# Column-tiled square sums with tokens on partitions, quartered input and transposed output in a two-layer streaming encoder

## What is computed

```python
def rmsnorm(x, g):
    y = x * lax.rsqrt(jnp.mean(x * x, axis=-1, keepdims=True) + EPS)
    return y * g

def ffn_half(x, g, wg, wu, wd):
    h = rmsnorm(x, g)
    return x + 0.5 * ((jax.nn.silu(h @ wg) * (h @ wu)) @ wd)

def layer(h, ...):
    h = ffn_half(h, n1, w1g, w1u, w1d)
    z = rmsnorm(h, nm) @ w_in
    m, st = token_mix(z, ...)      # chunk MLP, window attention, latent attention
    h = h + m @ w_out
    return ffn_half(h, n2, w2g, w2u, w2d), st
# two layers, then y = rmsnorm(h, norm_final)
```

## Time and profile before

| | |
|---|---|
| runs | 2149.73, 2156.65, 2157.35 us; median 2156.65 |
| the profiled execution's own time | 2156.49 us |
| its span, first to last instruction | 2154.7 us |
| mean granted TensorE clock | 0.992 of full |
| busy: PE, DVE, ScalarE, POOL | 97%, 65%, 43%, 26% |

### The profile page before, as it was taken

How to read it: one execution, slowest core, us unless ns; L and a number is a source line. 1 busy time by engine, 2 the same in 40 slices (tenths; PEclk the granted TensorE clock), 3 DMA queues, 4 the chain that set the end, 5 groups by cost and what they waited for, 6 DMA issues and landing times.

```text
span 2154.7 us, 40797 instructions
## 1 busy us (share of the span) xinstructions
PE 2094.6 (97%) x15625; PEld 2021.1 (94%) x15625; DVE 1410.2 (65%) x2115; ACT 917.7 (43%) x1654; POOL 562.7 (26%) x308
## 2 busy tenths in 40 slices
PE   8999999999998999999989999999999899999999
PEld 7999999998777999999989999999987799999998
DVE  7899961145646899972289999312465479999511
ACT  6444442224535544453255555322244364444411
POOL 2222223341112222223322221333312022222231
PEclk9999999999998999999999999999999999999999
DMA  4323323431112232322223332224222023332322
GB/s 127 98 79 96 95 74 85 110 90 44 42 42 79 68 92 94 97 81 81 75 79 98 97 97 76 81 84 115 69 56 52 30 61 96 97 97 76 91 83 70
DMA packets 250467, 175.37 MB, mean 81 GB/s; under 512 B 35408, under 2 KB 245552, under 8 KB 250352
## 3 DMA queue, kind: packets, MB, share of 16 engines
q1 hardware_dynamic: 248272, 170.09, 26.9%
q10 hardware_dynamic: 2080, 3.67, 0.5%
HBM read 170.12 MB, written 3.62 MB: 81 GB/s over the span
## 4 chain that ended last, share of the span: by engine, by line
PE 88%; DVE 6%; ACT 4%; issue 2%; DMA 0%; ACTq 0%; DVEq 0%
PE pair L1228 42%; PE pair L1179 36%; PE pair L1259 3%; PE pair L1434 1%; PE pair L1269 1%; ACT probs L1089 1%; ACT hidden_high L883 1%; DVE top L2013 1%; PE pair L1425 1%; PE pair L1420 1%; PE pair L1413 1%; PE pair L1376 1%; ACT square L762 1%; DVE t_parts L1870 0%; PE pair L1516 0%
## 5 line engine op out<-in xcount | busy, mean ns | idle before, releaser
L1228 PE MATMUL pair<-t_parts,chunk_high 128*128 128x288 f32 x4592 | 918.0, 296 | 8.7 <-DVE outputs L1680 5.6
L1228 PEld LDWEIGHTS pair<-t_parts,chunk_high 128*128 128x128 f32 x4592 | 738.9, 189 | 9.9 <-issue 7.0
L1228 PE MATMUL pair<-t_parts,chunk_low 128*128 128x288 f32 x2296 | 678.5, 296 | 0.0
L712 POOL TENSOR_TENSOR w_low<-raw,w_high 128x1024 fp32r<-128x1024 f32 (+1 forms) x128 | 294.2, 2308 | 772.6 <-ACT w_high L755 641.4
L1228 PEld LDWEIGHTS pair<-t_parts,chunk_low 128*128 128x128 f32 x2296 | 432.6, 188 | 0.0
L718 POOL TENSOR_TENSOR chunk_low<-set_raw,chunk_high 128x512 fp32r<-128x512 f32 x164 | 237.6, 1459 | 701.7 <-ACT chunk_high L807 701.7
L807 ACT ACTIVATE chunk_high<-chunk_sum 128x512 fp32r<-128x512 f32 x328 | 204.3, 631 | 388.3 <-DVE chunk_sum L1599 188.5
L1179 PE MATMUL pair<-hidden_high,w_high 128*128 128x288 f32 x1408 | 303.1, 297 | 6.6 <-DVE hidden_low L1805 6.2
L1179 PE MATMUL pair<-hidden_low,w_high 128*128 128x288 f32 x1408 | 301.4, 296 | 0.0
L1179 PE MATMUL pair<-hidden_high,w_low 128*128 128x288 f32 x1408 | 301.3, 296 | 0.0
L1565 DVE SCALAR_TENSOR_TENSOR outputs<-pair,rms 128x576 f32<-128x576 f32 x32 | 24.2, 758 | 371.2 <-PE pair L1179 371.2
(11 more groups left out here) (252 smaller groups left out, 2793.6 us busy)
## 6 DMA issues: line engine op xcount, KB each, us to landing
set_raw<-in_w_up_dram SPq DMA_DIRECT2D x44, 1024.0 KB, 5.3
set_raw<-in_w_gate_dram SPq DMA_DIRECT2D x44, 1024.0 KB, 5.3
raw<-in_w_down_dram SPq DMA_DIRECT2D x64, 512.0 KB, 3.8
raw<-in_w_down_dram SPq DMA_DIRECT2D x32, 384.0 KB, 3.5
raw<-in_w_in_dram SPq DMA_DIRECT2D x20, 512.0 KB, 3.9
raw<-in_w_in_dram SPq DMA_DIRECT2D x16, 256.0 KB, 3.8
raw<-in_w_out_dram SPq DMA_DIRECT2D x8, 512.0 KB, 3.5
raw<-in_w_out_dram SPq DMA_DIRECT2D x16, 256.0 KB, 4.1
```

The costliest lines, as they stand in the source:

```text
L712: nc.gpsimd.tensor_tensor(**low_of(s, slot_size(s))).then_inc(low_ready, 1)
L1228: mm = nc.tensor.matmul(out, c[:, j, p, :], tr[p // 2][:, p % 2, x, t, :], start=p == 0 and n == 0, stop=p == KP - 1 and n == 2)
```

## The change

- The mean square of a plain opening is made with 32 weight columns in each product. Square m goes to rows 32 (m mod 3) to 32 (m mod 3) + 31 of pair 3, so three partial sums lie in 96 rows. It now comes after tile (0,1). ScalarE copies the 96 rows to `rms`, and after tile (1,0) PE sums them with tokens on the partitions (5 products with one moving column into pair 0).
- Root and reciprocal are taken on `root_tok` [128, 5]. ScalarE's `spread` scales the identity by each token's value into `sq_tmp`, PE multiplies by `mean_d` (`FIRST` pair, or ALONE in layer 1's first phase), and `keep_scale` copies the result to `rms`, times 1024.
- `make_rms` becomes `make_scale` and moves in DVE's order. DVE waits for `rms_spread` before its first use of `rms`. In the normal opening `mean_square` is one step, `spread_scale` follows S4 and A22 of set (0,1), and set (1,0) waits for `rms_spread` at A11; `after_plain` now holds for plain phases only.
- The low parts of weight tiles (0,0), (1,0), (1,1) move from POOL to DVE (`plain_chunk_low`); POOL only passes the counts on. Tile (0,0) takes its records pair by pair.
- x comes in four quarters, the sample rows in one transfer on SP's queue; ScalarE copies h's even tiles whole, DVE the odd ones; w_up's load waits for the third quarter, w_gate's for the fourth. Three fp32 products of `sq_sum` (zeros) run on PE ahead of the transposes.
- DVE multiplies the last h by the gain into `y_in`, and `y_chunk` is a plain transpose; `diag` goes.

```diff
+            sp.dma_start(x_tok[0:DEC, 4, :], a["x_sample"][0]).then_inc(x_sample_in, 16)
...
-                    sp.wait_ge(x_in[0], 32)
+                    sp.wait_ge(x_in[2], 16)
...
-                        sp.wait_ge(xT_done, KD)
+                        sp.wait_ge(x_in[3], 16)
...
                 for n in range(2):
+                    if b == 0 and n == 0:
+                        pool.wait_ge(plain_low, 3 * plain_before(layer, w) + 1)
+                        pool.sem_inc(low_by_pool, 1)
+                        continue
+                    if b == 1:
+                        pool.wait_ge(plain_low, 3 * plain_before(layer, w) + n + 2)
+                        pool.wait_ge(low_by_pool, 2 * q + n)
+                        pool.sem_inc(low_by_pool, 1)
+                        continue
                     pool.wait_ge(chunk_high, 7 * q + (3, 7)[n])
...
-                    nc.scalar.activation(rms[:, half * HALF:(half + 1) * HALF], ps[ALONE][:, 1, 0:HALF], ACT.Sqrt,
-                                         bias=eps[:, 0:1]).then_inc(root_done, 1)
+            def root(count, sums, parts):
+                act.wait_ge(sum_done, 2 * count + 2)
+                nc.scalar.activation(root_tok[:, 0:4], sums[:, 0:4], ACT.Sqrt, bias=eps[:, 0:1], scale=float(parts)).then_inc(root_done, 1)
+                nc.scalar.activation(root_tok[0:DEC, 4:5], sums[0:DEC, 4:5], ACT.Sqrt, bias=eps[0:DEC, 0:1], scale=float(parts)).then_inc(root_done, 1)
+            def spread(count):
+                act.wait_ge(rms_ready, count + 1)
+                for t, (t0, n) in enumerate(TILES):
+                    ins = nc.scalar.activation(sq_tmp[0:n, t0:t0 + n], ident[0:n, 0:n], ACT.Copy, scale=root_tok[0:n, t:t + 1])
+                ins.then_inc(spread_made, 1)
+            def keep_scale(ph, part, pair, half):
+                act.wait_ge(scale_made, 2 * ph + part + 1)
+                dst, src = (rms[:, 0:SEQ], ps[pair][:, 0, :]) if part == 0 else (rms[:, SEQ:NT], ps[pair][:, half, 0:DEC])
+                nc.scalar.activation(dst, src, ACT.Copy, scale=float(D_MODEL)).then_inc(rms_spread, 1)
             def gate_up(layer, w, base_slot):
                 ph = 2 * layer + w
...
                     for j in (S1, S2, S3, S4):
                         chunk(q + 1, 1 - b, j)
+                        if opens and b == 1 and j == S1:
+                            spread(3 * layer + 2 * w)
+                        if opens and b == 1 and j == S4:
+                            keep_scale(ph, 0, ALONE, 0)
                     done(A22)
                     chunk(q + 1, 1 - b, A22)
+                    if opens and b == 1:
+                        keep_scale(ph, 1, ALONE, 0)
                 if is_plain(layer, w):
...
+                keep_up(0)
                 combined_of(0)
+                act.wait_ge(sum_done, 2 * ph + 1)
+                nc.scalar.activation(two(rms[0:96, :]), halves(3)[0:96], ACT.Copy).then_inc(parts_kept, 1)
...
-                keep_up(0)
+                keep_up(1)
                 combined_of(2)
+                root(ph, ps[ALONE][:, 0, 0:5], D_MODEL // 32)
                 combined_of(3)
-                act.wait_ge(sum_done, 2 * ph + 2)
-                nc.scalar.activation(two(rms[:, :]), halves(3), ACT.Sqrt, bias=eps[:, 0:1]).then_inc(root_done, 2)
+                spread(3 * layer + 2 * w)
                 chunk(q + 2, 0, A11)
                 chunk(q + 2, 0, A12)
-                keep_up(1)
-                for j in (S1, S2, S3, S4):
+                for j in (S1, S2):
+                    chunk(q + 2, 0, j)
+                keep_scale(ph, 0, FIRST, 0)
+                keep_scale(ph, 1, FIRST, 1)
+                for j in (S3, S4):
                     chunk(q + 2, 0, j)
...
-            for f in range(2):
...
-                act.dma_start(x_tok[0:DEC, 4, c], a["x_sample"][0, :, c]).then_inc(x_in[f], 16)
-            def sample_part(m):
...
             def ahead_of_first(m):
...
-                    after_plain = isinstance(i, int) and i == 1 and b == 0
+                    after_plain = isinstance(i, int) and i == 1 and b == 0 and is_plain(layer, w)
...
+                            if isinstance(i, int) and i == 1 and b == 0 and not is_plain(layer, w):
+                                pe.wait_ge(rms_spread, 2 * ph + 2)
+                        if j == A12 and after_plain:
+                            pe.wait_ge(rms_spread, 2 * ph + 2)
...
+                            mean_square()
+                        if opens and b == 1 and j in (S4, A22):
+                            spread_scale(int(j == A22))
+                def mean_square():
+                    pe.wait_ge(sq_added, 2 * KD * layer + 1)
...
+                        for t0, n in TILES[:4]:
+                            mm = nc.tensor.matmul(ps[ALONE][:, 0, t0:t0 + n], mean_d[:, :], sq_tmp[:, t0:t0 + n], start=True, stop=True)
                     else:
-                        pe.wait_ge(root_done, 2 * ph + 1)
-                    nc.tensor.matmul(ps[ALONE][:, 1, 0:HALF], mean_d[:, :], sq_sum[:, half * HALF:(half + 1) * HALF],
-                                     start=True, stop=True).then_inc(sum_done, 1)
+                        pe.wait_ge(rms_spread, 2 * ph + 1)
+                        mm = nc.tensor.matmul(ps[ALONE][:, 0, 0:DEC], mean_d[0:DEC, :], sq_tmp[0:DEC, SEQ:NT], start=True, stop=True)
+                    mm.then_inc(scale_made, 1)
                 def plain_tile(b, n):
                     q = set_number(layer, w, 0, b)
                     pe.wait_ge(h_ready, x_count + (5 + 2 * b + n))
-                    pe.wait_ge(low_by_pool, 2 * q + (n + 1))
...
+                    elif b == 1:
+                        pe.wait_ge(plain_low, 3 * plain_before(layer, w) + n + 2)
+                    else:
+                        pe.wait_ge(low_by_pool, 2 * q + (n + 1))
+                    arrival = b == 0 and n == 0
+                    order = [(e, p) for p in range(KP) for e in range(2)] if arrival else [(e, p) for e in range(2) for p in range(KP)]
...
                                 for signal, count in ((t_ready[B21], ph * KP),) if e else ((t_ready[B11], ph * KP), (b12_ready, plain_before(layer, w) * KP)):
                                     pe.wait_ge(signal, count + (p + 1))
                             for k, (c, x) in enumerate(((ch, 0), (ch, 1), (cl, 0))):
                                 for half in range(2):
...
+                    plain_tile(0, 1)
                     pe.wait_ge(sq_made, x_count + KD)
                     pe.wait_ge(h_ready, x_count + KD)
-                    for n, src in enumerate(squares):
+                    for turn in range(3):
                         for half in range(2):
-                            mm = nc.tensor.matmul(ps[3][:, half, 0:HALF], mean_d[:, :], src[:, half * HALF:(half + 1) * HALF],
-                                                  start=n == 0, stop=n == KD - 1)
-                    mm.then_inc(sum_done, 2)
-                    plain_tile(0, 1)
+                            for m in range(3 * turn, min(3 * turn + 3, KD)):
+                                r = slice(m % 3 * 32, (m % 3 + 1) * 32)
+                                mm = nc.tensor.matmul(ps[3][r, half, 0:HALF], mean_d[:, 0:32], squares[m][:, half * HALF:(half + 1) * HALF],
+                                                      start=turn == 0, stop=m + 3 >= KD)
+                    mm.then_inc(sum_done, 1)
                     plain_tile(1, 0)
+                    pe.wait_ge(parts_kept, plain_before(layer, w) + 1)
+                    pe.wait_ge(left_made, set_number(layer, w, 0, 0) + 1)
+                    for t, (t0, n) in enumerate(TILES):
+                        mm = nc.tensor.matmul(ps[ALONE][0:n, 0, t:t + 1], rms[0:96, t0:t0 + n], mean_d[0:96, 0:1], start=True, stop=True)
+                    mm.then_inc(sum_done, 1)
                     plain_tile(1, 1)
+                    pe.wait_ge(root_done, 2 * ph + 2)
+                    pe.wait_ge(spread_made, ph + 1)
+                    pe.wait_ge(left_made, set_number(layer, w, 0, 0) + 2)
+                    for t, (t0, n) in enumerate(TILES):
+                        dst = ps[FIRST][:, 0, t0:t0 + n] if t < 4 else ps[FIRST][:, 1, 0:n]
+                        mm = nc.tensor.matmul(dst, mean_d[0:n, :], sq_tmp[0:n, t0:t0 + n], start=True, stop=True)
+                    mm.then_inc(scale_made, 2)
                     one_set(1, 0)
...
+            pe.wait_ge(const_made, 2)
+            for n in range(3):
+                nc.tensor.matmul(ps[0][:, 0, 0:HALF], sq_sum[:, 0:P], sq_sum[:, 0:HALF], start=True, stop=True)
...
+                    if t == 0 and m % 2 == 0:
+                        pe.wait_ge(x_in[m // 2], 16)
+                    if t == 4 and m == 0:
+                        pe.wait_ge(x_sample_in, 16)
...
                 down(layer, 1, F2D, 2)
...
+                return nc.tensor.transpose(dst, y_in[:, m, t0:t0 + n], ident[:, :])
             for t in range(3):
```

(31 more changed lines are left out.)

83 lines of the change are left out of this document (42 added, 41 removed).

## The result

The changed kernel takes 2142.60 us (median of 2141.17, 2141.83, 2143.37 and 2143.92), the kernel before 2156.97 beside it: a ratio of 0.9938, with an interval of 0.9923 to 0.9954. So it is faster; that it is faster by more than 0.5% isn't certain, as the interval ends on the other side of 0.995. One of the six executions of `f1_combined`, a kernel of the experiments, took 5153.45 us; it is left out there, and the median is that of the other five.

What follows compares the result with a forecast made beforehand. PE, busy 97% of a 2154.7 us span, was taken as the bound. Gains of 3.8 + 2 x 2.7 + 4.9 + 2.5 = 16.6 us from 2156.5 gave 2140 us; 8-in-10 range 2133 to 2152.

Steps and rivals of the forecast that it cites:

- Squares 4.6 us: Mean square in each of three plain openings: three column groups overlap partly, 4.6 us instead of 8.03, saving 3.4.
- Spread 1.1 us: Five spreading products on PE, 576 columns in all, add 1.1 us per opening.
- New wait 1.0: Plain openings: PE waits 1.0 us at A11, whose chunk and POOL low stand behind the spread on ScalarE.
- First tile without a stall, 2.6 us: Plain openings at 667 and 1726: pair-by-pair records end the 1.9 us wait for lows; tile ends 2.6 us sooner.
- Layer 1's opening 4.9 us: Layer 1's first phase, without plain tiles: 2.4 us from the reciprocal and L1680 wait gone, 2.5 from slow clock gone.
- The first opening 3.8 us: Program start: x in quarters starts PE sooner, first tile ends 3.7 us earlier; with squares and new work, 3.8 us gained.
- Tail 2.5 us: Program end: plain transposes 0.11 us apart, sums 1.3 us sooner, last eviction at 2147.1 instead of 2149.62: 2.5 us gained.
- Untouched stretches 0: Long stretches between the openings keep their instructions, so no gain or loss was booked there: 0.
- A: Rival: column tiles do not overlap, squares stay at 8.0 us, 10.3 us lost: 2150 us; chance 0.14.
- B: Rival: threefold overlap, squares 3.0 us, and the new waits hidden: 2132 us; chance 0.16.
- C: Rival: the PE, ScalarE, DVE hand-over ahead of A12 becomes the bound, 5.6 us in each opening: 2164 us; chance 0.06.
- D: Rival: start gains nothing, tail falls to slow spacing, layer 1's waits keep the clock low: 2148 us; chance 0.14.

Runs made afterwards that it cites:

- f1_combined: Changed kernel with ScalarE's keep_scale copies earlier, no products ahead of the transposes, gain rows second on SP's queue, sample rows behind x's first quarter: 2139.91 us (0.9923).
- c2_keep_early: Changed kernel with ScalarE's order in plain openings: A11, scaled identity copies, A12, both keep_scale copies, then S1 to S4: 2140.10 us (0.9923).
- b1_condition: Kernel before with only after_plain limited to phases with plain tiles; the 128x576 reciprocal stays: 2151.32 us (0.9978).
- h1_w_up_sooner: f1_combined with SP's first w_up load issued on x's second quarter in place of its third: 2138.75 us (0.9926).
- a2_two_groups: Changed kernel with the squares in two column groups, four turns of two, in place of three turns of three: 2145.25 us (0.9951).
- d1_no_warm: Changed kernel without the three products ahead of the first transposes: 2139.97 us (0.9930).
- g1_four_times: Changed kernel with the last token tile's eight transposes made four times each: 2143.64 us, a single execution.

## Why the prediction was right, and where it was not

The time (2142.6 for 2140, in the range) and the sign are right, and so is the reason for most of it: the column groups, the order of arrival, the condition. Most sizes were not, and that the sum came so near is in part luck: by the table the start gave 3.0 us less than forecast, the tail 1.3 less and the untouched stretches 2.7 less, and the three other openings 3.0 more. Of the signs that I named, the waits of about 1 us, the vanished wait for L1680 and the 0.11 us of the transposes were seen; the squares in 4 to 5 us were not.

- *Squares 4.6 us:* they take 3.03. The step that failed is "only neighbours' halves overlap, so that a third group adds little". One, two and three groups at 7.87, 4.00 and 3.03 us show each turn at the price of one product. It was an assumption put between two bounds, and the lower bound was the truth: 1.6 us in each of three openings. The 8.03 that I started from was 0.4 too long for this use, so the saving is 4.6 us where I booked 3.4. The Trainium skill (TensorE: Matmul & The Clock Gate, Part 3) gives 2.38 times for three column tiles of 512 moving columns; here, with 288, it is 7.87 / 3.03 = 2.6, with two of the eight products left over for the last turn.
- *Spread 1.1 us:* 1.49. I scaled by columns. In layer 1's opening the four products of 128 columns take 0.81 us (L1292 at 1101.30, the next record at 1102.11), less than the 0.9 of the scaling; the five of a plain opening take 1.43, so the fifth, of 64 rows and 64 columns, costs 0.6. *Sums 1.16:* measured 1.16. *New wait 1.0:* 0.73, and at the place named, A11, behind the spread on ScalarE; `c2_keep_early` shows it gone with the order.
- *First tile without a stall, 2.6 us:* the mechanism is right and shown by the old order's 2.1 us of waiting. By rows it is 2.3: before, 8.90 us from the tile's first record (677.67) to the squares (686.57), now 12.98 with a second tile of 6.35. The wait for the lows was 1.9 of it; most of the rest is a wait for the squares, which PE had in each of the three openings (0.7 us in all, the longest 0.3) and has no more.
- *Layer 1's opening 4.9 us:* 6.2. The waits were 0.86 and 0.41 us instead of 0.9, 1.3 and 0.8: S4 didn't wait for `spread_made` at all. The stall and the slow clock behind it went, as forecast, and `b1_condition` puts 5.5 of it on the condition. My sum was also 0.4 off: 1107.4 less 0.5, with 1.1, 0.9, 1.3 and 0.8 added, is 1111.0 and not 1110.6.
- *The first opening 3.8 us:* 0.8, the largest miss. Its failed step is "issued on x's third quarter at about 8": that quarter landed at 10.4, so `w_up` was 3.4 us later than in the kernel before and its first high part began at 16.04. I had let the chunk's low be ready at 17.0, with the load landing at 14.3; it was ready at 19.64. The load, landing at 15.95, accounts for 1.65 us of that. The other 1.0 is an order that I left out: DVE's low doesn't follow the high part (ready at 17.10) but the lows of h's fifth tile, whose high parts stand behind it on ScalarE, and so it starts at 18.42. The wait for the gain rows (1.7 us) was longer than my bound of 1.3, but transposes that end 1.2 to 1.45 us sooner gave 0.2 us, since ScalarE then waited for the load. Against the forecast 2.85 us of start are missing (19.85 for 17.0), and the longer slow spacing takes another 1.3 (5.9 us of it for 3.3, half lost); the shorter squares give 1.6 back.
- *Tail 2.5 us:* 1.2. The sums began 1.26 us sooner, as forecast. The last eviction ended 2.4 sooner, as forecast, and it didn't matter: "the last eviction" was the wrong end. The output's transfer takes 8.1 us from the first issue to the end, and that issue came 1.2 us sooner. The window of the earlier trace rows had shown it (DMA share 1.01) and I read only its clock. That the clock may fall there is borne out by four of the traces, but at 0.50 the transposes of `h1_w_up_sooner` stand 0.21 us apart, not the 0.27 that I took, and the end didn't move.
- *Untouched stretches 0:* -2.7. Largest, from 1122 to the last opening, with 4542 PE records in each; first the whole, then its end (before, then after):

```profile
1122.00:1736.70 614.70, 599.92 (x4542) 569.97 (x4541) 379.90 (x595) 265.04 (x498) 160.73 (x82) 0.99 0.27 77
1705.00:1736.70 31.70, 26.89 (x196) 23.36 (x195) 17.82 (x37) 14.12 (x33) 5.91 (x4) 0.84 0.22 67
```
```profile
1112.00:1728.60 616.60, 601.22 (x4542) 571.07 (x4541) 380.01 (x597) 265.45 (x499) 158.91 (x81) 0.99 0.26 76
1695.00:1728.60 33.60, 28.77 (x197) 24.52 (x198) 17.73 (x39) 14.88 (x33) 3.55 (x2) 0.80 0.19 63
```

  1.3 us are the same records at a slower pace, 0.8 a longer wait for ScalarE's roots in the attention. The end of the stretch has all of it: there the granted clock is 0.50 for some 10 us before and 14 after. Both lengths stand in traces of kernels that have the change (some 10 in `a2_two_groups`, `d1_no_warm`, `g1_four_times` and `h1_w_up_sooner`, 14 in the others), so the change alone doesn't decide it; whether it has a part in it stays open.

Of the rivals, A (no overlap) is out: the groups share their rows and still overlap. C (the hand-over as the bound) is out as well; by its own price of 2164 it was within 0.5% of the kernel before, and so not the case "slower" that its chance was booked under. B was right on the squares and wrong on the waits, D nearly right on the start.

What no run here separates: the quarters of x from the sharing of the copies, and the plain transposes of the tail from its new order. Both were read from the two traces alone.

## What to carry to other kernels

Small-column products of independent operands can go to several column groups in turn: each turn then costs one product, and the merging of the groups can be left to a product that is needed anyway. Before an engine's copy or a wait is made cheaper, look at what the wait stands for: one superfluous condition was worth more here than the faster reciprocal it seemed to ask for. At both ends of a program, ask first what the DMA queues do: a tail whose transfers run at full rate ended the same 8.1 us after its first issue whatever the engines did behind it, and a load that waits for a later piece of a split transfer goes out later than it did.

## What the runs showed of the hardware

- Column groups: 16 fp32 products of 288 columns in 7.87, 4.00 and 3.03 us with one, two and three groups; the products of a turn start within 0.02 us, and all groups read the same 128 rows.
- Transposes of 128x128 fp32 take 0.27 us each at the start and 0.11 in the tail (21 in 2.46). In the changed kernel the windows from 10 to 20 us show a granted clock of 0.50, the 1.2 GHz level, those of the tail 1.00. But the clock alone doesn't make the 0.27: in the tail of `h1_w_up_sooner` the same transposes stand 0.21 us apart at 0.50. What slows them further at the start was not tried. In the kernel before the same 0.27 stood in windows that show 1.00, so at the start that column doesn't tell the pace, and the records' spacing does.
- An fp32 product of 64 rows and 64 columns costs some 0.6 us on PE's path among products of 128 rows, three times one of 128 columns (0.20). What of it is the change of the rows in use was not tried.
